# Fewer recurrence tiles beside the cached pages, and a short first group of dense tokens

## The chip, the cores and the metric

One core of a Trainium2 chip runs the whole kernel. The metric is the device time of one execution, in microseconds. TensorE (PE in the profile) does the matrix products and writes to PSUM; PEld is its loading of weights. VectorE is DVE, ScalarE is ACT, GpSimd is POOL. SyncE (SP) computes nothing: it issues most of the DMAs, one after the other, and waits before each for what it needs.

## The reference, cut to what matters

One layer of a hybrid decoder, run on a prompt of 2048 tokens and on 8 samples of 4 new tokens each, in 32-bit floats:

- `cols = RMSNorm(x) @ w_in`, split among three head groups.
- Gated delta rule (6 heads of 64): a causal convolution, then a recurrence over chunks of 64 tokens that carries a 64x64 state for each head. Called GDN below.
- Differential attention (4 heads): causal on the prompt; for the samples over 64 cached pages of 128 rows each, found through a page table.
- RWKV7 (6 heads of 64): a second recurrence with a 64x64 state for each head.
- `x += concat(three outputs) @ w_out`; then attention to 256 memory tokens; then a gated feed-forward of width 2816 with a causal convolution of width 3 on the gate; then a final RMSNorm. Caches and states are outputs too.

The recurrences are serial over token tiles. All that follows `w_out` is independent from token to token, but for the convolution, which needs the two tokens before.

## The kernel before, in words

The program is written out by hand. Each piece of work is a *lane*: one Python generator for each engine, which issues the instructions of one slot and yields. The functions `weave` (slots spread evenly) and `merge` (slots put at given places) interleave the lanes of several pieces into one fixed order of instructions on each engine. Engines execute in that order, so a slot that waits holds up all that was put behind it on its engine. Semaphores tie the engines together.

The stages, in order of time:

1. Projection and the prompt's attention (0 to about 1254 us).
2. **Cached pages.** `paged_lanes` reads 512 pages of keys and 512 of values, 128 KB each. SP issues three of four key pages and a part of the value pages, ACT and POOL the rest. Beside it, woven in, run the first `LEAD` token tiles (of 128 tokens) of GDN, then the first `LEAD` of RWKV, then the projection of the memory tokens (`in_turn`, lines 4256 to 4270). `paged_lanes` has 162 slots, a GDN tile 24, an RWKV tile 29, the memory projection 15; both sides are spread evenly over the stage.
3. The recurrences of the samples (to about 2095 us).
4. **Dense groups.** `feed_lanes` takes the 2080 tokens in five groups of `GROUPS` columns. Each group passes all weights once: `op` (w_out, 8 units), `wq`, `sc`/`nrm`/`tp`/`pv` (memory attention, in four sub-tiles of `quarter(c)` tokens), `wo`, `fp` (feed-forward up, 11 quads of 7 units), `fo` (down, 24 units), `ft` (final norm and stores, again by sub-tiles). The `fp` units multiply halves of the group (one level of Strassen: 7 products instead of 8), so their matmuls have `GROUPS[c]/2` columns. A unit's weights are one tile of at most 512 KB, in a ring of `W_RING` = 4. Merged in are the remaining token tiles of both recurrences: `spread` (line 4384) gives each group the tiles that the next group will read, evenly over its own places up to unit `fo` 14. Group 4 has none; the samples' memory attention and closing transposes stand there. `tokens_done` makes SP wait for the tiles' stores before a group's input is loaded.

`GROUPS` sets the shape of two kinds of transfer. With q = `quarter(c)`, a group's tokens are cut in four sub-tiles of q rows (the last group adds one of 32, the samples):

```python
quarter = lambda c: (GROUPS[c] - (NS if c == NCH - 1 else 0)) // 4
...
sp.dma_start(xs[0:q, n % 2, 0:4, :],
             pr.i["x_prompt"][0][t0:t0 + q * 4, at].rearrange("(i p) n -> p i n", p=q))
...
dst = pr.y_p[GROUP_AT[c] + at:GROUP_AT[c] + at + n, :] if n > NS else pr.y_s
sp.dma_start(dst, res[0:n, j % 2, :]).then_inc(stored[j % 2], 16)
```

The first (line 3420) loads the residual input, q partitions of four rows of 512 bytes, once for each `op` unit, two buffers. The second (line 3450) stores a finished sub-tile, n rows of 4096 bytes, from two buffers: ACT fills a buffer again only when its store has landed (`act.wait_ge(stored...)` in `ft`). At the end of the last group these stores are the last work of the program.

Of the kernel before, what the change touches and what calls it, by code (L numbers as in the profile page):

```python
# [39 lines left out]
NEG = -1.0e30  # L40


LEAD = 3
GROUPS = (384, 384, 416, 448, 448)
W_RING = 4
GROUP_AT = tuple(sum(GROUPS[:c]) for c in range(len(GROUPS)))
GROUP_P = GROUPS[-1] - NS
B_QKV, B_Z, B_DIFF, B_RWKV, B_BETA = 0, 9, 12, 18, 29
# [3214 lines left out]
def feed_lanes(nc, st, pr, C):  # L3263
    L = Lanes()
    GM, NA, RING = max(GROUPS), 9, W_RING
    Q = 112
    PARTS = (range(0, 8), range(8, 16), range(16, 22))
    quarter = lambda c: (GROUPS[c] - (NS if c == NCH - 1 else 0)) // 4

# [51 lines left out]
    spare = lambda c: xTs[:, (c + 1) % 2, :, :].rearrange("p k n -> p (k n)")  # L3321
    prob_of = lambda c, j: spare(c)[0:Q, 1024 * (j % 2):1024 * (j % 2) + 1024].rearrange("p (h m) -> p h m", m=MEM)

    def pT_of(c, j):
        cells = spare(c)[:, 2048:2048 + 8 * Q] if j % 2 == 0 else flat[:, 4 * GM:4 * GM + 8 * Q]
        return cells.rearrange("p (c h n) -> p c h n", c=2, h=MH)
    res = flat[0:Q, NA * GM - 2048:NA * GM].rearrange("p (u d) -> p u d", u=2)
    rstd = st.sb("f_rstd", [P, GM])
# [18 lines left out]
    def tokens(c):  # L3347
        G, H = GROUPS[c], GROUPS[c] // 2
        sums_of = lambda n: spare(c)[:, n * 2 * GM:(n + 1) * 2 * GM].rearrange("p (k n) -> p k n", k=4)[:, :, 0:H]
        one, two = slice(0, H), slice(H, G)  # L3350
        return dict(a11=h[:, 0:4, one], a12=h[:, 4:8, one], a21=h[:, 0:4, two], a22=h[:, 4:8, two],
                    s1=sums_of(0), s2=sums_of(1), s3=h[:, 0:4, two], s4=sums_of(2))

    def temps(c):
        H = GROUPS[c] // 2
        return [spare(c)[:, (6 + n) * GM:(7 + n) * GM].rearrange("p (a n) -> p a n", a=2)[:, :, 0:H] for n in range(2)]
# [112 lines left out]
    def pe_lane(pe):  # L3469
        def step(c, kind, j):  # L3470
# [48 lines left out]
            if kind == "tp":  # L3519
# [3 lines left out]
                for x in range(2):  # L3523
                    u = (kind, c, 2 * j + x)
                    free(pe, u)
                    for hh in range(MH):
                        mm = pe.transpose(bank(u)[:, hh * Q:hh * Q + n], prob[0:n, hh, x * P:(x + 1) * P], pr.ident[0:n, 0:n])
                    mm.then_inc(E.sem[kind], 1)
            if kind == "pv":
# [4 lines left out]
                for hh in range(MH):  # L3534
                    for x in range(2):
                        mm = pe.matmul(bank(u)[:, hh * Q:hh * Q + n], C.mV[:, x, hh * MHD:(hh + 1) * MHD], pT[:, x, hh, 0:n],  # L3536
                                       start=(x == 0), stop=(x == 1))
# [34 lines left out]
    def act_lane(act):  # L3572
# [14 lines left out]
        def step(c, kind, j):  # L3587
# [26 lines left out]
            if kind == "tp":  # L3614
# [5 lines left out]
                for x in range(2):  # L3620
                    u = (kind, c, 2 * j + x)
                    E.wait(act, "tp", c, 2 * j + x)
                    act.activation(pT[:, x, :, 0:n], bank(u)[:, 0:4 * Q].rearrange("p (h n) -> p h n", n=Q)[:, :, 0:n], ACT.Copy)\
                       .then_inc(E.sem["ptk"], 1)
# [208 lines left out]
def memory_lanes(nc, st, pr, F, banks, recurrences):  # L3833
# [24 lines left out]
    def clear(eng):  # L3858
        for lane in recurrences:
            eng.wait_ge(lane.stored, 16 * (TILES - LEAD))  # L3860

# [106 lines left out]
def closing_lanes(nc, st, pr, C, F, banks, recurrences, jobs, stores, f_rows, f_stores):  # L3968
# [8 lines left out]
    def clear(eng):  # L3977
        for lane in recurrences:
            eng.wait_ge(lane.stored, 16 * (TILES - LEAD))

# [51 lines left out]
def build(nc, ins, outs, upto=99):  # L4032
# [12 lines left out]
    with Stage(nc) as st:  # L4045
# [22 lines left out]
        with Stage(nc) as ds:  # L4068
# [131 lines left out]
            with Stage(nc) as ms:  # L4200
# [51 lines left out]
                with Stage(nc) as ps:  # L4252
                    K_ = paged_lanes(nc, ps, pr, A_)
                    banks = [ps.ps(f"shared{j}", [P, 512]) for j in range(3)]
                    with Shared(ps, banks) as gs:
                        D_ = gdn_lanes(nc, gs, pr, S_g, C, 0, LEAD)
                    with Shared(ps, banks) as rs_:
                        R_ = rwkv_lanes(nc, rs_, pr, S_r, C, 0, LEAD)
                    with Shared(ps, banks) as ms_:
                        W_ = memory_project_lanes(nc, ms_, pr, C, g_kv)  # L4260
                    loads_in, r_in = ps.sem("loads_in"), ps.sem("r_in")
                    done = ((D_.stored, 16 * LEAD), (r_in, 16 * len(r_loads)))
                    n_slots = D_.slots + R_.slots + W_.slots
                    last = ((R_.stored, 16 * LEAD),)
                    turns = lambda eng, one, two, three: (
# [84 lines left out]
                with Stage(nc) as ls:  # L4350
# [6 lines left out]

                    C.tokens_done = tokens_done
                    F_ = feed_lanes(nc, ls, pr, C)
                    banks = [ls.ps(f"bank{j}", [P, 512]) for j in range(6)]  # L4360
                    with Shared(ls, banks) as first:
# [121 lines left out]
```

## Time and profile before

| what | value |
|---|---|
| runs, median of 3 | 5283.54 us (5266.91 to 5286.02) |
| the profiled execution, its own time | 5274.61 us |
| its span, first to last instruction | 5273.0 us |
| PE busy | 4786.2 us, 91% of the span |
| PE weight load busy | 3456.9 us, 66% |
| DVE busy | 2540.1 us, 48% |
| ACT / POOL busy | 1408.7 us, 27% / 837.3 us, 16% |
| TensorE's mean granted clock | 0.943 of full |
| HBM read / written | 541.70 MB / 72.16 MB |

The profile is one execution, and all rows below come from it. A busy share over the whole span mixes stages with different limits, so the rows are taken by stage.

### The profile page before, as it was taken

Reading aid. Unit: us, or ns where it says so; the run is one execution under the profiler, and the core shown is the slowest. Engines: PE = TensorE matmul, PEld = TensorE weight load, DVE = VectorE, ACT = ScalarE, POOL = GpSimd, SP = SyncE. Lnnn points to the kernel's source line nnn. Section 1 sums busy time; section 2 is a strip of 40 time slices with the busy share of each in tenths; the row PEclk is TensorE's granted clock in tenths of the full one; section 3 lists DMA queues with packets and bytes.
Section 4 is the critical chain, followed back from the end, with each engine's and each line's share of the span. In section 5 each row is a group of like instructions: output and inputs, shape, how many; then the busy total and the mean of one; then the engine's idle time right before and its main releaser. Section 6 shows DMA issues by size and latency. Waiting matters only on the chain. (4 is left out here: it accounts for less than half of the span.)

```text
span 5273.0 us, 99191 instructions
## 1 busy us (share of the span) xinstructions
PE 4786.2 (91%) x38490; PEld 3456.9 (66%) x38490; DVE 2540.1 (48%) x5724; ACT 1408.7 (27%) x3230; POOL 837.3 (16%) x1111
## 2 busy tenths in 40 slices
PE   8888999997777878999999999989999899999998
PEld 5544445554545555687776877768776597757885
DVE  1136666663445524466545655446453464412442
ACT  3224544552223312222213222132121321112111
POOL 3422221212232210111011110210101101010000
PEclk9999999998888875999999999989999899997999
DMA  6631111114777733144342433424443243342443
GB/s 214 223 98 34 40 37 37 39 37 124 217 230 234 240 116 68 54 138 130 122 119 63 137 123 120 123 56 143 124 125 102 64 135 105 123 146 72 152 143 96
DMA packets 684224, 620.34 MB, mean 118 GB/s; under 512 B 82759, under 2 KB 637255, under 8 KB 683724
## 3 DMA queue, kind: packets, MB, share of 16 engines
q1 hardware_dynamic: 610990, 517.16, 32.6%
q10 hardware_dynamic: 60480, 63.27, 3.7%
q0 software_dynamic: 12288, 33.57, 2.1%
q8 instruction: 307, 5.03, 0.4%
q14 instruction: 159, 1.30, 0.1%
HBM read 541.70 MB, written 72.16 MB: 116 GB/s over the span
## 5 line engine op out<-in xcount | busy, mean ns | idle before, releaser
L3485 PE MATMUL s_f_b<-s_arena 128*128 128x192 f32 (+2 forms) x3520 | 668.5, 346 | 14.3 <-DVE s_arena L3673 7.7
L3485 PEld LDWEIGHTS s_f_b<-s_arena 128*128 128x128 f32 x3520 | 620.4, 192 | 33.2 <-issue 18.3
L3555 PE MATMUL s_f_b<-s_f_a,s_arena 128*128 128x384 f32 (+2 forms) x1760 | 635.0, 517 | 1.5 <-DVE s_f_a L3721 1.5
L581 PE MATMUL s_p_acc<-s_hT,s_p_W 128*128 128x416 f32 x1600 | 606.5, 526 | 6.5 <-DMA s_p_W<-in_w_in_dram 6.5
L3555 PEld LDWEIGHTS s_f_b<-s_f_a,s_arena 128*128 128x128 f32 x1760 | 330.0, 191 | 264.5 <-issue 173.9
L3485 PE MATMUL s_f_b<-s_f_xT,s_arena 128*128 128x192 f32 (+2 forms) x2640 | 495.7, 342 | 0.1
L3485 PEld LDWEIGHTS s_f_b<-s_f_xT,s_arena 128*128 128x128 f32 x2640 | 460.0, 190 | 8.5 <-issue 1.4
L581 PEld LDWEIGHTS s_p_acc<-s_hT,s_p_W 128*128 128x128 f32 x1600 | 297.9, 195 | 245.6 <-issue 232.0
L3495 PE MATMUL s_f_b<-s_arena 128*128 128x384 f32 (+2 forms) x960 | 355.6, 524 | 12.4 <-PEq L124 9.3
L3769 DVE TENSOR_TENSOR s_f_xT<-s_f_xT,s_f_b 128x384 f32<-128x384 f32 (+2 forms) x160 | 93.9, 587 | 498.7 <-PE s_f_b L3555 423.4
L3817 POOL TENSOR_TENSOR s_f_ex<-s_f_ex,s_f_mix 128x384 f32<-128x384 f32 (+2 forms) x105 | 112.2, 1069 | 1272.5 <-ACT s_f_mix L3585 1272.3
L3495 PEld LDWEIGHTS s_f_b<-s_arena 128*128 128x128 f32 x960 | 180.8, 193 | 156.1 <-issue 108.9
L934 ACT ACTIVATE s_prob<-s_s_ps,s_ntop 128x512 f32<-128x512 f32 (+3 forms) x320 | 196.4, 620 | 303.7 <-DVE s_ntop L989 303.6
L3658 ACT ACTIVATE s_f_ex<-s_f_ex 128x384 f32<-128x384 f32 (+2 forms) x110 | 60.5, 550 | 488.4 <-DVE s_f_ex L3707 488.4
L1224 PE MATMUL s_tp<-s_ident,s_K 128*128 128x128 f32 x1024 | 162.7, 307 | 27.7 <-DMA s_K<-in_cache_diff_k_dram 13.4
L1198 POOL DMA_DIRECT2D s_arena<-in_cache_diff_v_dram x256 | 138.8, 542 | 258.5 <-issue 256.3
L986 DVE TENSOR_REDUCE s_ntop<-s_s_ps 128x2 f32<-128x1024 f32 (+3 forms) x160 | 169.7, 1060 | 20.0 <-PE s_s_ps L878 17.7
L1224 PEld LDWEIGHTS s_tp<-s_ident,s_K 128*128 128x128 f32 x1024 | 128.8, 157 | 48.7 <-issue 17.2
L878 PE MATMUL s_s_ps<-s_kT,s_qT 32*128 32x512 f32 (+3 forms) x640 | 82.9, 588 | 69.9 <-ACT s_prob L934 69.8
L1066 POOL TENSOR_SCALAR s_prob<-s_prob,s_alpha 128x512 f32<-128x512 f32 (+3 forms) x160 | 102.4, 654 | 249.3 <-DVE s_alpha L1016 246.0
L3219 POOL TENSOR_TENSOR s_g_zg<-s_g_zt,s_norm_g 128x384 f32<-128x384 f32 x16 | 17.4, 1087 | 769.5 <-DVE s_g_o L3103 738.0
L1412 DVE COPY s_kT<-s_tp 128x512 f32<-128x512 f32 x128 | 88.1, 688 | 87.1 <-PE s_tp L1224 86.5
(813 smaller groups left out, 8069.4 us busy)
## 6 DMA issues: line engine op xcount, KB each, us to landing
s_arena<-w_sums SPq DMA_DIRECT2D x220, 512.0 KB, 3.3
s_arena<-in_ffn_w_in_dram SPq DMA_DIRECT2D x165, 512.0 KB, 3.6
s_K<-in_cache_diff_k_dram SPq DMA_DIRECT2D x384, 128.0 KB, 3.1
s_arena<-in_ffn_w_out_dram SPq DMA_DIRECT2D x80, 512.0 KB, 4.0
s_arena<-in_cache_diff_v_dram POOLq DMA_DIRECT2D x256, 128.0 KB, 3.8
s_arena<-in_cache_diff_v_dram ACTq DMA_DIRECT2D x192, 128.0 KB, 3.6
s_parts<-in_ffn_w_in_dram SPq DMA_DIRECT2D x88, 256.0 KB, 4.4
w_sums<-s_parts SPq DMA_DIRECT2D x44, 512.0 KB, 2.9
```

Source lines behind the costliest of these rows:

```text
L581: mm = pe.matmul(self.acc[n % 2][:, 0:CH], self.W[:, u, k, :], self.hT[:, k, c * CH:(c + 1) * CH], start=(k == 0), stop=(k == KD - 1))
L934: e = act.activation(prob[:, slot(n, c), r, 0:wd], s_ps[hh][:, m, 0:wd], ACT.Exp, scale=scale, bias=ntop[:, u, c, r:r + 1], accum_out=den[ ...
L986: dve.tensor_reduce(ntop[:, u, c, 2 * hh:2 * hh + 2], s_ps[hh][:, :, 0:wd], AX.X, ALU.max)\
L1066: m = pool.tensor_scalar(prob[:, k, 2 * hh + 1, 0:wd], prob[:, k, 2 * hh + 1, 0:wd], alpha[:, n % 2, c, 2 * hh + 1:2 * hh + 2], 1.0, ALU.m ...
L1198: pool.dma_start(V_[:, g % VG, i, :], vp[page_of(pool, g, i)].rearrange("a p h d -> p (a h d)"))\
L1224: mm = pe.transpose(dst[:, i, :], K[:, g % KG, i, h * P:(h + 1) * P], pr.ident[:, :])
L1412: dve.tensor_copy(kT[:, g % 6, 1, :], src[:, :, :].rearrange("p i n -> p (i n)"))\
L3485: mm = pe.matmul(out[:, x, :], w[:, k, x, :], right[:, k, :], start=(k == 0), stop=(k == 3))
L3495: mm = pe.matmul(bank(u)[:, 0:G], w[:, k, :], h[:, k, 0:G], start=(k == 0), stop=(k == KD - 1 and kind != "op"))
L3555: mm = pe.matmul(bank(u)[:, 0:G], w[:, k, :], a[:, f % NA, 0:G], start=(k == 0), stop=(k == len(part) - 1))
L3769: dve.tensor_tensor(x, x, bank(u)[:, 0:G], ALU.add).then_inc(E.sem[kind + "k"], 1)
L3817: pool.tensor_tensor(acc, acc, sq[:, m % 2, 0:GROUPS[c]], ALU.add).then_inc(E.sem["add"], 1)
```

## The change

The number of token tiles of each recurrence that run beside the cached pages goes from three to two; the third tile of GDN and the third of RWKV run in the dense stage. The groups become one of 256 tokens and four of 456. `Q`, the stride of a head in the banks of the memory attention, follows the largest sub-tile.

```diff
-LEAD = 3
-GROUPS = (384, 384, 416, 448, 448)
+LEAD = 2
+GROUPS = (256, 456, 456, 456, 456)
...
 def feed_lanes(nc, st, pr, C):
     L = Lanes()
     GM, NA, RING = max(GROUPS), 9, W_RING
-    Q = 112
+    Q = 114
```

What follows from it by the code's own arithmetic: the sub-tiles `quarter(c)` go from 96, 96, 104, 112, 104 rows to 64, 114, 114, 114, 106. The token tiles that `spread` puts beside groups 0 to 3 go from 3, 4, 3, 3 to 4, 4, 3, 3. The slots woven against the 162 of the cached pages go from 174 to 121. No function is added.

## Rows read from the trace of the kernel before

**Rows 1.** Windows by stage: length, busy (instructions) of each engine, PE clock, DMA, GB/s.
```profile
1254.00:1917.00 663.00, 486.24 (x6409) 339.95 (x6409) 304.87 (x649) 169.83 (x323) 191.46 (x312) 0.85 0.73 219
1917.00:2095.00 178.00, 142.88 (x943) 107.95 (x943) 63.23 (x160) 26.40 (x74) 6.84 (x11) 0.65 0.35 73
2095.00:5250.00 3155.00, 3031.45 (x26110) 2366.96 (x26110) 1535.53 (x3433) 688.78 (x1494) 328.84 (x325) 0.97 0.37 113
```

**Rows 2.** Waits of SyncE, 1254 to 1770 us: total us, times, longest.
```profile
SPq L1154 <- PE s_tp L1224: 32.9, 17, 7.9
```

**Rows 3.** The same in 1270 to 1470 us.
```profile
SPq L1154 <- PE s_tp L1224: 1.0, 2, 0.8
```

**Rows 4.** SyncE's issues in order of time: six key pages.
```profile
1409.99 5.85 SPq L1161 DMA_DIRECT2D s_K<-in_cache_diff_k_dram  x6
```

**Rows 5.** The recurrences' banks in the stage of the pages, same columns, no POOL.
```profile
1269.00:1900.00 631.00, 160.71 (x3544) 131.62 (x3544) 79.87 (x186) 34.14 (x73) 0.86 0.74 223
```

**Rows 6.** End of the stage in order of time: last RWKV output, memory projection's first matmul.
```profile
1907.72 0.49 ACT L2650 ACTIVATE s_r_oT<-s_shared 128x384 f32<-128x384 f32 x1 [4.42 <-PE s_shared L2639]
1917.57 1.94 PE L1578 MATMUL s_shared<-s_ident,s_w_x 128*128 128x128 f32 x8 [9.89 <-ACT s_w_x L1566]
```

**Rows 7.** The recurrences' banks beside groups 0 to 3, 13 tiles of each.
```profile
2095.00:4666.00 2571.00, 599.05 (x15431) 511.99 (x15431) 343.18 (x806) 152.90 (x325) 0.98 0.37 111
```

**Rows 8.** The dense banks in group 0 (384 tokens) and group 4 (448).
```profile
2095.00:2728.00 633.00, 457.89 (x2036) 340.47 (x2036) 66.68 (x121) 23.77 (x65) 0.98 0.37 113
4666.00:5272.00 606.00, 524.71 (x2102) 390.40 (x2101) 74.31 (x121) 36.76 (x85) 0.93 0.39 120
```

**Rows 9.** Runs of matmuls at full clock with 192, 224 and 128 columns.
```profile
2331.01 5.47 PE L3485 MATMUL s_f_b<-s_arena 128*128 128x192 f32 x32
4931.99 6.22 PE L3485 MATMUL s_f_b<-s_arena 128*128 128x224 f32 x32
1953.57 14.46 PE L1589 MATMUL s_shared<-s_w_W,s_w_mT 128*128 128x128 f32 x128
```

**Rows 10.** Ends of two GDN tiles that follow each other fastest, in group 1.
```profile
2777.28 0.47 ACT L3048 ACTIVATE s_g_oT<-s_bank 128x384 f32<-128x384 f32 x1
2908.26 0.49 ACT L3048 ACTIVATE s_g_oT<-s_bank 128x384 f32<-128x384 f32 x1
```

**Rows 11.** That stretch: all engines.
```profile
2777.00:2908.00 131.00, 117.55 (x1498) 85.13 (x1496) 78.04 (x173) 44.23 (x112) 25.43 (x25) 0.97 0.23 64
```

**Rows 12.** PE's waits there: longest in total, and the largest by a recurrence.
```profile
PE s_f_b L3508 <- POOL s_f_ex L3817: 7.3, 2, 4.8
PE s_bank L2431 <- ACT s_r_rs L2650: 1.0, 1, 1.0
```

**Rows 13.** DMA, 5254 to 5267 us: packets, queue with share of 16 engines, issues.
```profile
DMA packets 516, 1.84 MB, mean 141 GB/s; under 512 B 68, under 2 KB 68, under 8 KB 516
q1 hardware_dynamic: 516, 1.84, 50.7%
out_dram<-s_f_a SPq DMA_DIRECT2D x4, 416.0 KB
out_dram<-s_f_a SPq DMA_DIRECT2D x1, 128.0 KB
```

**Rows 14.** DMA, 1970.5 to 1973.5 us: two stores of 128 partitions alone.
```profile
DMA packets 544, 1.05 MB, mean 350 GB/s; under 512 B 32, under 2 KB 32, under 8 KB 544
q1 hardware_dynamic: 544, 1.05, 93.8%
```

**Rows 15.** DMA, 4666 to 4718 us, the `op` units of group 4, packets of 512 bytes.
```profile
q1 hardware_dynamic: 10142, 5.05, 36.6%
```

**Rows 16.** Two `op` units of group 4, and the last stores, in order of time.
```profile
4665.76 6.28 PE L3495 MATMUL s_f_b<-s_arena 128*128 128x448 f32 x16
4673.18 6.28 PE L3495 MATMUL s_f_b<-s_arena 128*128 128x448 f32 x16
5254.74 9.49 SPq L3450 DMA_DIRECT2D out_dram<-s_f_a  x5
```

## The prediction

> **What bounds the kernel now.** I read the busy table by stage first, then in each stage the waits of the engine that issues or computes last, then the transfers at the end.
>
> In the dense stage PE is busy 3031 of 3155 us [rows 1]: whatever is added to PE there is paid in full. In the stage of the cached pages PE is busy 486 of 663 us, DMA 73% of its time, DVE less than half [rows 1], so none of these fills it. SP does nearly: six key pages take 5.85 us from the first start to the last end [rows 4], 1.1 us a page, so that its 384 key and 64 value pages are 493 us, before the states and tiles that it loads too. What SP waits for PE before it gives out a page is 32.9 us in 516 [rows 2], and 1.0 us in the 200 from 1270 on [rows 3]. The stage is paced by SP's issues most of the time and by PE the rest. After the last page a serial piece stands alone: the last RWKV output at 1907.7 us, its store, and the memory projection's first matmul at 1917.6, 9.9 us idle [rows 6].
>
> **The change part by part.** All against the profiled execution (5274.6 us; the median of the runs is 8.9 us above it).
>
> *One tile of each recurrence leaves the pages.* Three tiles cost PE 160.7 us there at a mean clock of 0.86 [rows 5], one 53.6. What that gives back is bounded by who paces. From below: if SP's issues set all, only the tile's own loads and the overlap at the end, some 15 us. From above: all of PE's 53.6 us, a third of its stalls on recurrence results (20, an estimate: of its 175 idle us in the stage about a third), and the end piece, some 90 us. Between: SP's waits for PE are 33 us, of which I take 25, since one third of the woven work goes but the order keeps the rest; the stretch after the last key page, where the RWKV chain and the last values' products alternate, has a third fewer RWKV slots in it, 8 us; and the last tile now ends before slot 142 of 162, beside the products of the last pages, so that its closing norm and store, ahead of the 9.9 us idle [rows 6], are half hidden, 10 us. I take 43 us less, the ends being 15 and 90.
>
> *The tile arrives in the dense stage.* 599.05 us for 13 tiles [rows 7] are 46.1 us of PE each, on an engine with no room: plus 46 us.
>
> *Closer recurrence slots in group 0.* Dense work on PE is 457.9 us at 384 tokens and 524.7 at 448 [rows 8], 1.04 us a token with little fixed beside 57 us; 256 tokens come to about 325. Up to unit `fo` 14, some 86% of it by the units' count of matmuls, group 0 is then 280 us and four tiles of 46: 464 us, 116 us a tile, where the same sum gives 177 for three tiles before. The fastest tile in the trace took 131 us [rows 10], and there PE was idle 13.4 us [rows 11], of which the largest wait on a recurrence is 1.0 and the largest of all, 7.3, is the group's own sum of squares [rows 12]. DVE was busy 60% there. So the chains can run at that spacing; for 10% closer I add 2 us a tile, 8 us, between 0 and 40 (10 us a tile, what the woven recurrences show in the stage of the pages at 105 us a tile).
>
> *Other matmul widths.* The pitch is 5.47/32 = 171 ns at 192 columns, 194 at 224, 113 at 128 [rows 9]; the loads of weights hide at 128 too. The columns streamed are the same in sum (1040 halves), and 113 + 4 x 197 is 901 against 171 + 171 + 182 + 194 + 194 = 912, times 1232 matmuls: 13 us less at best, nothing if the pitch at 228 is 200. I take 0. A weight tile of 512 KB then lasts 16 x 113 ns = 1.8 us on PE in group 0, but with the recurrence slots between some 3 us, and with three loads ahead that is hidden; uncovered it would be up to 2 us a tile of the 77.
>
> *Rows that don't divide.* Here stands the one cost outside PE's sum. In the last 13 us the only transfers are four stores of 104 rows and one of 32, and beside 448 packets of 4096 bytes (4 x 104 + 32) there are 68 small ones [rows 13]. With one closing packet for each DMA engine used, two stores of 128 partitions have 32, 16 each [rows 14]; 68 is 4 x 13 + 16. So 104 rows went over 13 engines, 8 rows each, and 32 over 16: the number is one that divides the rows, the largest up to 16. For 114 rows it is 6, for 106 it is 2. The Trainium skill, "DMA: Bandwidth & Descriptors", section "Why a DMA increments its semaphore by 16 and not by 1", says just this: the largest k up to 16 that divides the slowest dimension of both sides. By that rule the sum is the one below; the trace agrees (68 small packets).
>
> - The last four stores: 50.7% of 16 engines over 13 us is 105 us for 516 packets, 204 ns each [rows 13]; two stores alone ran at 45 us for 544 packets of 2048 bytes, 83 ns, or 165 for 4096 [rows 14]. Four stores of 53 packets on each of two engines are 212 x 165 to 204 ns = 35 to 43 us, and ACT's next sub-tile waits for them, two buffers behind. The first is issued at 5254.7 us [rows 16], and all five are over before 5267 [rows 13], 9 to 10 us of flow for what will take 35 to 43: plus 26 to 34 us, I take 30. Nothing is left beside it to hide it.
> - The residual loads of group 4: packets of 512 bytes take 0.366 x 16 x 52 / 10142 = 30 ns [rows 15]. 106 rows are 212 packets on each of two engines, 6.4 us, and these also carry 64 of each weight tile, 1.9: 8.3 us for an `op` unit that lasts 7.4 [rows 16] and will last 7.55. Eight units: 6 us, less what the two buffers absorb; I take 3, between 0 and 20.
> - With 114 rows a store is 19 packets on an engine, 4 us, and a load 76 x 30 ns = 2.3 us; both are hidden in groups 1 to 3, where the sub-tiles are spread between other units.
>
> **Sum:** -43 + 46 + 8 + 0 + 30 + 3 = +44 us, 5319 us for the profiled execution; halfway to the runs' median, 5323 us.
>
> **The rivals.**
>
> A. *The thin stores don't come.* 106 rows go over many engines by some other split. For it: only 104, 128 and 32 were seen. Against: 8 rows on each of 13 engines instead of 7 on 15 is a split that nobody would choose but by divisors. Sum +11, 5290 us.
>
> B. *Group 0 is bound by its chains.* Up to `fo` 14, 40% of PE's time there would be recurrence against 26% before; DVE does the two convolutions of a quad in one go, and a recurrence result queued behind them comes too late for PE's next slot. If each of the four tiles loses 14 us more, the sum is +100, 5379 us. For it: a tile every 105 us is all that the stage of the pages reaches, with one recurrence at a time. Against: PE's waits in the fastest tile [rows 11, 12].
>
> C. *The pages were paced by PE.* The stage gives back 90 us or more, with the clock (0.85 there) recovering. Against 46 for the tile and 26 for the stores it turns the sign from 72 us on; at 100 us, no stalls in group 0 and 26 for the stores the sum is -25, 5254 us, faster. Against: SP hardly waits for PE in the first 200 us of pages [rows 3].
>
> **How the numbers follow.** The forecast 0.66, its own range 5290 to 5350; A 0.13; B 0.13; C 0.08. What the measurement can tell from no change is 0.5%, 26 us: 5257 to 5310. Of the forecast 0.54 lies above, of B all, of A a little: slower 0.69. Same 0.25 (the rest of the forecast and most of A), faster 0.06. The range 5280 to 5370 leaves out C, the top of B and a little of the rest.
>
> **What would show it.** The stage of the pages ends 30 to 55 us earlier; if under 20, SP alone paced it, if over 75, C. From the first `op` copy of group 0 to the next group's about 560 us (was 633), with PE idle under 40; over 70 is B. PE busy in the banks of the recurrences over groups 0 to 3 is 645 us. In the last 60 us: four stores of 424 KB with few small packets (4 x 2 + 16 = 24), DMA at 2/16 of its engines, ACT waiting for the stores about 10 us each, and from the first of them to the end some 48 us (was 18). If the small packets are 76 or more, the split is another and A holds.

## The result, and the profile after

The changed kernel takes 5369.9 us (median; 5354.8 to 5378.5) against 5284.8 us of the kernel before in the same comparison: 1.0164 times as long, 95% interval 1.0139 to 1.0189. The profiled execution has a span of 5376.9 us, 103.9 us more than before's 5273.0. The forecast was 5323 us: slower, as measured, but by 38 us, less than half of the measured 85.

Where the span grew, by windows of the profile after (length, busy time and instructions of PE, PEld, DVE, ACT and POOL, granted clock, DMA share, GB/s). The first line is cached pages with the samples' recurrences, then groups 0 to 4, each from its first `op` copy on ACT:

```profile
1248.30:2047.20 798.90, 577.79 (x6175) 401.78 (x6175) 320.56 (x699) 177.06 (x352) 181.37 (x306) 0.80 0.67 196
2047.20:2674.20 627.00, 554.29 (x7743) 485.47 (x7741) 365.64 (x904) 160.71 (x378) 97.66 (x105) 0.92 0.39 118
2674.20:3391.60 717.40, 689.89 (x6582) 522.74 (x6583) 381.70 (x817) 168.24 (x353) 92.26 (x89) 0.98 0.34 103
3391.60:4074.80 683.20, 659.26 (x5636) 496.74 (x5639) 334.89 (x710) 148.80 (x308) 73.99 (x72) 0.98 0.35 106
4074.80:4729.00 654.20, 631.71 (x4909) 475.96 (x4909) 304.60 (x640) 132.04 (x271) 57.03 (x55) 0.97 0.34 106
4729.00:5376.90 647.90, 582.81 (x2472) 445.79 (x2471) 204.82 (x489) 108.51 (x241) 24.08 (x21) 0.91 0.36 112
```

The same six windows of the kernel before:

```profile
1241.40:2095.00 853.60, 629.15 (x7353) 447.90 (x7352) 370.72 (x822) 197.26 (x399) 198.30 (x323) 0.80 0.64 187
2095.00:2728.00 633.00, 610.27 (x6563) 485.61 (x6564) 347.71 (x781) 151.20 (x331) 87.48 (x88) 0.98 0.37 113
2728.00:3379.50 651.50, 619.46 (x6586) 493.27 (x6590) 362.54 (x817) 160.59 (x354) 88.94 (x89) 0.98 0.37 113
3379.50:4021.20 641.70, 615.59 (x5637) 477.89 (x5638) 323.65 (x710) 144.45 (x309) 72.10 (x72) 0.98 0.37 112
4021.20:4665.90 644.70, 622.64 (x4909) 474.53 (x4910) 301.83 (x640) 131.12 (x272) 56.66 (x55) 0.98 0.35 107
4665.90:5273.00 607.10, 572.03 (x2471) 441.52 (x2471) 202.66 (x489) 107.05 (x241) 23.66 (x21) 0.93 0.39 120
```

Read length minus PE busy as PE's idle time. The pages are 54.7 us shorter. Group 0 has two thirds of the tokens and is only 6 us shorter: its idle time went from 22.7 to 72.7 us and its clock from 0.98 to 0.92. Groups 1 to 3 carry more tokens, with as little idle time as before (73.9 us against 80.2). Group 4 has 65.1 us idle against 35.1. What stands before the pages ended 6.9 us later, with the same instructions; in all eighteen profiles of this document it ends between 1237.3 and 1251.5 us, so this is scatter.

What PE waited for in group 0 (line, releaser, total us, times, longest), the six largest:

```profile
PE s_bank L2639 <- DVE s_r_o L2720: 13.8, 4, 3.8
PE s_f_b L3485 <- DVE s_f_val L3796: 13.6, 3, 6.3
PE s_bank L2584 <- DVE s_r_APk L2792: 8.6, 2, 4.7
PE s_f_b L3527 <- DVE s_f_a L3759: 5.5, 1, 5.5
PE s_bank L2969 <- DVE s_g_kq L3103: 4.6, 3, 3.1
PE s_bank L3037 <- DVE s_g_o L3103: 4.0, 3, 2.7
```

All six end on DVE, though DVE is busy only 58% of the group: 50.1 us, five of them on recurrence work or on a bank whose release stands behind it. In group 0 of before the first of these was 3.9 us and the second was not in the list.

By banks, the recurrences in group 0 and in groups 1 to 3 (answering [rows 7]), then the dense banks in groups 0 and 4 (answering [rows 8]):

```profile
2047.00:2674.00 627.00, 224.02 (x5710) 190.12 (x5706) 124.75 (x292) 57.59 (x121) 0.92 0.39 118
2674.00:4729.00 2055.00, 428.09 (x10905) 367.12 (x10905) 245.14 (x576) 107.77 (x229) 0.98 0.34 105
2047.00:2674.00 627.00, 347.11 (x2036) 296.26 (x2036) 51.54 (x121) 20.45 (x65) 0.92 0.39 118
4729.00:5376.00 647.00, 531.04 (x2103) 390.45 (x2102) 75.25 (x121) 37.18 (x85) 0.91 0.36 112
```

The fourteenth tile brought 53.1 us (652.1 against 599.05).

The last stores, DMA from 5330 us to the end (packets, queue share of 16 engines, issues), and what ACT's copies into the two row buffers waited for:

```profile
DMA packets 481, 1.88 MB, mean 40 GB/s; under 512 B 24, under 2 KB 24, under 8 KB 480
q1 hardware_dynamic: 480, 1.87, 10.6%
out_dram<-s_f_a SPq DMA_DIRECT2D x4, 424.0 KB
out_dram<-s_f_a SPq DMA_DIRECT2D x1, 128.0 KB
```

```profile
5344.71 1.09 ACT L3653 ACTIVATE s_f_a<-s_f_b 106x512 f32<-106x512 f32 x2 [8.99 <-DMA out_dram<-s_f_a]
5352.96 1.08 ACT L3653 ACTIVATE s_f_a<-s_f_b 106x512 f32<-106x512 f32 x2 [7.16 <-DMA out_dram<-s_f_a]
5361.19 1.07 ACT L3653 ACTIVATE s_f_a<-s_f_b 32x512 f32<-32x512 f32 x2 [7.15 <-DMA out_dram<-s_f_a]
```

24 small packets are 4 x 2 + 16, where [rows 13] had 68: two DMA engines for a store of 106 rows, sixteen for 32. The copies come 8.2 us apart, 155 ns for each of 53 packets. From the first of the last stores to the end it is 42.9 us, against 18.2.

### The profile page after: what moved, and what is told of

The parts are those of the page before. It is cut to its first block and busy times, and to the rows that moved or that the text cites. A ratio compares the mean times of both kernels' runs of the same rounds, so it can differ in the third digit from the quotient of the medians.

```text
span 5376.9 us, 99189 instructions
## 1 busy us (share of the span) xinstructions
PE 4821.9 (90%) x38490; PEld 3469.3 (65%) x38490; DVE 2543.3 (47%) x5724; ACT 1412.8 (26%) x3230; POOL 836.9 (16%) x1111
## 5 line engine op out<-in xcount | busy, mean ns | idle before, releaser
L3485 PE MATMUL s_f_b<-s_arena 128*128 128x228 f32 (+1 forms) x3520 | 676.1, 349 | 27.0 <-DVE s_f_val L3796 15.8
L3555 PE MATMUL s_f_b<-s_f_a,s_arena 128*128 128x456 f32 (+1 forms) x1760 | 635.9, 517 | 1.4 <-DVE s_f_a L3721 1.4
L3485 PE MATMUL s_f_b<-s_f_xT,s_arena 128*128 128x228 f32 (+1 forms) x2640 | 499.8, 344 | 0.8 <-ACT s_f_xT L3633 0.8
L3495 PE MATMUL s_f_b<-s_arena 128*128 128x456 f32 (+1 forms) x960 | 360.2, 530 | 14.6 <-PEq L124 9.3
L3769 DVE TENSOR_TENSOR s_f_xT<-s_f_xT,s_f_b 128x456 f32<-128x456 f32 (+1 forms) x160 | 94.0, 588 | 532.1 <-PE s_f_b L3555 443.1
L3817 POOL TENSOR_TENSOR s_f_ex<-s_f_ex,s_f_mix 128x456 f32<-128x456 f32 (+1 forms) x105 | 111.9, 1066 | 1232.5 <-ACT s_f_mix L3585 1232.5
L3658 ACT ACTIVATE s_f_ex<-s_f_ex 128x456 f32<-128x456 f32 (+1 forms) x110 | 60.4, 549 | 487.8 <-DVE s_f_ex L3707 487.8
L3219 POOL TENSOR_TENSOR s_g_zg<-s_g_zt,s_norm_g 128x384 f32<-128x384 f32 x16 | 17.4, 1088 | 817.4 <-DVE s_g_o L3103 786.1
L1285 PE MATMUL s_o_ps<-s_arena,s_PT 128*32 128x256 f32 x1024 | 82.2, 475 | 61.2 <-DMA s_arena<-in_cache_diff_v_dram 60.5
```

Source lines behind the costliest of these rows:

```text
L3485: mm = pe.matmul(out[:, x, :], w[:, k, x, :], right[:, k, :], start=(k == 0), stop=(k == 3))
L3495: mm = pe.matmul(bank(u)[:, 0:G], w[:, k, :], h[:, k, 0:G], start=(k == 0), stop=(k == KD - 1 and kind != "op"))
L3555: mm = pe.matmul(bank(u)[:, 0:G], w[:, k, :], a[:, f % NA, 0:G], start=(k == 0), stop=(k == len(part) - 1))
L3769: dve.tensor_tensor(x, x, bank(u)[:, 0:G], ALU.add).then_inc(E.sem[kind + "k"], 1)
L3817: pool.tensor_tensor(acc, acc, sq[:, m % 2, 0:GROUPS[c]], ALU.add).then_inc(E.sem["add"], 1)
```

## Experiments

All against the kernel before on the same chip; "own" is the median. The kernel before had a median of 5275.0 to 5284.8 us in these comparisons, so a difference of two "own" times carries up to 10 us of that; the ratios don't. Group 0's length and PE idle time are from each kernel's profile.

| run | own us | ratio, 95% interval | group 0 us | idle us |
|---|---|---|---|---|
| the change | 5369.9 | 1.0164 (1.0139 to 1.0189) | 627.0 | 72.7 |
| e1 split stores | 5340.8 | 1.0111 (1.0088 to 1.0135) | 626.6 | 67.2 |
| e2 and split loads | 5349.3 | 1.0130 (1.0107 to 1.0153) | 625.4 | 70.9 |
| e3 narrow taps | 5359.2 | 1.0147 (1.0123 to 1.0170) | 617.1 | 64.0 |
| e4 LEAD 3, new groups | 5333.7 | 1.0099 (1.0074 to 1.0124) | 527.4 | 32.0 |
| e5 before, LEAD 4 | 5328.0 | 1.0086 (1.0069 to 1.0103) | 575.9 | 17.9 |
| e7 before, 106-row tail | 5313.9 | 1.0070 (1.0053 to 1.0086) | 632.8 | 22.7 |
| e9 before, slots squeezed | 5317.2 | 1.0075 (1.0058 to 1.0092) | 664.0 | 46.0 |
| e10 no convolution | 5357.7 | 1.0153 (1.0136 to 1.0170) | 613.8 | 63.0 |
| e11 = e1, convolutions apart | 5339.2 | 1.0094 (1.0071 to 1.0118) | 628.9 | 62.7 |
| e12 = e1, slots spread | 5341.0 | 1.0112 (1.0091 to 1.0134) | 584.9 | 54.2 |
| e13 = e4, split stores | 5310.8 | 1.0053 (1.0036 to 1.0071) | 527.4 | 30.3 |
| e14 = e13, LEAD 4 | 5354.0 | 1.0140 (1.0118 to 1.0162) | 466.6 | 23.1 |
| e15 = e1, half a slot apart | 5366.9 | 1.0156 (1.0134 to 1.0178) | 630.7 | 71.2 |
| e16 before, half a slot apart | 5317.0 | 1.0067 (1.0049 to 1.0084) | 649.2 | 30.5 |
| e17 = e1, more dense work | 5367.7 | 1.0175 (1.0144 to 1.0207) | 655.2 | 40.7 |
| e18 before, more dense work | 5378.4 | 1.0185 (1.0164 to 1.0205) | 731.1 | 19.8 |

### The thin transfers: e1, e2, e7

```diff
-                sp.dma_start(dst, res[0:n, j % 2, :]).then_inc(stored[j % 2], 16)
+                cuts = [0, 96, n] if c == NCH - 1 and n > 96 else [0, n]
+                for lo, hi in zip(cuts, cuts[1:]):
+                    sp.dma_start(dst[lo:hi, :], res[lo:hi, j % 2, :]).then_inc(stored[j % 2], 16)
```

(the waits on `stored` count two for one in the last group; e2 cuts the loads of line 3420 in the same way; e7 is the kernel before with `GROUPS = (384, 384, 416, 440, 456)`.)

> The kernel after, with each 106-row store of the last group given out as two, of 96 and of 10 rows. Theory 1 (a store of 106 rows is served by 2 DMA engines, and the last sub-tiles wait for it): the stretch from the first of the last stores to the end falls from 43 us to 15 to 20 us, ACT's 23 us of waits for a free row buffer go, and the time is 24 to 30 us less than that of the kernel after, about 5343 us. Rival (the tail is long for another reason, as the lower clock there): less than 8 us, 5362 us or more. Nothing before the last sub-tiles changes.

> As the run with split stores, and the eight 106-row loads of residual x of the last group also in two parts, 96 and 10 rows. If those loads held PE up (my term was 3 us, 0 to 20), it is 3 to 9 us faster than with the stores split alone; if they are hidden, the same within 2 us, or a little slower for eight more issues on SP.

> The kernel before with the last two groups 440 and 456 tokens instead of 448 and 448, so that the last group's sub-tiles have 106 rows (and group 3's 110), nothing else. Theory (2 DMA engines for 106 rows): the stretch from the first of the last stores to the end grows from 18 to 43 us, the time by 24 to 30 us, 5299 to 5305 us. Rival (the tail costs so only together with the other group sizes or the moved tile): within 8 us of the kernel before.

Theory 1 held in e1: 29.1 us faster than the change, and from the first of the last stores to the end 17.7 us. DMA of e1's last 20 us:

```profile
DMA packets 577, 1.88 MB, mean 94 GB/s; under 512 B 120, under 2 KB 120, under 8 KB 576
q1 hardware_dynamic: 576, 1.87, 32.6%
```

The same bytes, and 120 small packets: 4 x 16 for 96 rows, 4 x 10 for 10, 16 for 32. In e7 the tail alone was put on the kernel before: 42.9 us from the first of the last stores, the same 23.3 us of ACT's waits as after the change, and the time is 34 us up, 4 to 10 more than I expected. The residual loads (the 106-row loads of line 3420) were hidden: with them split too, group 4's idle time is 40.4 us against 41.6. The time is no better; it is 8.5 us up, more than the 2 us I had allowed, but the two intervals overlap, and in the profiles PE's busy time in group 4 makes up the difference (591.6 against 581.0 us, at a clock of 0.91 against 0.93).

### The number of tiles beside group 0: e4, e13, e14, e5

One line each: `LEAD = 3` (e4, e13) or `LEAD = 4` (e14) in the changed kernel, `LEAD = 4` in the kernel before (e5). e13 and e14 have the split stores, so they compare with e1.

> Three tiles of each recurrence beside the pages as in the kernel before, with the groups of the kernel after (256, 456 x4): 3 tiles instead of 4 in the 256 tokens of group 0, and the thin transfers of the last group stay. Theory (density in group 0 costs the excess): PE idle in group 0 falls from 73 to about 40 us, mean clock there to 0.95 or more, banks of s_f_b in group 0 from 347 to about 335 us; against the kernel before +30 for the stores, +3 for the loads, about +15 for group 0: 5325 to 5335 us. Rival (a group of 256 tokens is costly by itself, whatever stands beside it): idle in group 0 stays above 60 us and s_f_b there at 345, 5355 us or more.

> The groups 256 and four of 456 with three tiles beside the pages and split stores: both named costs gone, the moved tile and the thin stores. If these two (29 us for the stores, 36 for the moved tile) add up, 5333.7 - 29 = 5305 us; what is left against the kernel before, 20 to 30 us, would be the group sizes themselves and what the rows of the runs show of the clock there. If they overlap, above 5315 us.

> Groups of 256 and four of 456, split stores, four tiles of each recurrence beside the pages: 2 tiles beside group 0, where 3 took 527.4 us and 4 took 626.6 us for the group, PE idle 30.3 and 67.2 us. Theory D (the price climbs as the slots close up): the step from 2 to 3 tiles is 50 to 60 us, against 99 from 3 to 4, so group 0 takes 467 to 477 us with 18 to 26 us idle. Rival (each tile costs the same 99 us in a group this narrow): 430 to 440 us. The stage of the pages grows by about 100 us as in the other run with four tiles there; total 5340 to 5360 us.

> The kernel before with four tiles of each recurrence beside the pages instead of three, groups unchanged: group 0 has 2 tiles beside it. From the two LEAD values measured so far with equal groups (a tile in the pages 55 to 66 us, in a crowded group 0 about 100, in an uncrowded one about 46 plus its stalls): if a tile's price in the dense stage is what its neighbours leave it, here where group 0 is roomy a tile moved out gives back only 46 to 55 us and costs 55 to 66 in the pages, 5275 to 5295 us. If the pages still had room for it (my term of 43 us for a tile) it would be even or faster, 5262 to 5275 us.

Group 0 of 256 tokens with two, three and four tiles beside it (e14, e13, e1), all engines; then for each the recurrences' banks and the dense ones:

```profile
2209.00:2675.60 466.60, 443.48 (x5376) 390.82 (x5375) 263.84 (x665) 121.06 (x290) 65.97 (x72) 0.97 0.50 150
2209.00:2675.60 466.60, 128.18 (x3339) 108.12 (x3339) 72.26 (x168) 33.92 (x71) 0.97 0.50 150
2209.00:2675.60 466.60, 329.33 (x2037) 283.91 (x2036) 51.42 (x121) 20.20 (x65) 0.97 0.50 150
```

```profile
2097.50:2624.90 527.40, 497.13 (x6552) 436.68 (x6552) 313.45 (x781) 138.67 (x331) 81.65 (x88) 0.95 0.45 136
2097.50:2624.90 527.40, 175.40 (x4516) 148.88 (x4516) 98.18 (x230) 45.42 (x96) 0.95 0.45 136
2097.50:2624.90 527.40, 339.04 (x2036) 288.55 (x2036) 51.39 (x121) 20.24 (x65) 0.95 0.45 136
```

```profile
2042.00:2668.60 626.60, 559.45 (x7742) 489.79 (x7738) 365.47 (x904) 160.23 (x378) 97.74 (x105) 0.92 0.39 118
2042.00:2668.60 626.60, 228.45 (x5706) 193.24 (x5702) 124.70 (x292) 57.36 (x121) 0.92 0.39 118
2042.00:2668.60 626.60, 347.73 (x2036) 297.30 (x2036) 51.48 (x121) 20.51 (x65) 0.92 0.39 118
```

The third tile costs 60.8 us (53.7 of PE's busy time, 7.1 idle), the fourth 99.2 (62.3 busy, 36.9 idle). The third lines hold one and the same dense work, and it takes 329.3, 339.0 and 347.7 us as the clock falls from 0.97 to 0.92: the stalls also make the work behind them slower, as the longest one below shows in single rows. This is the price of the step that failed. It is not the price of a narrow group, as e4's rival had it. Taking the stores as known, e1 against e13 is the move of the tile alone: 30 us slower (36 from e4 to the change), 99.2 us more in group 0 against 64 less in the stage of the pages. e13's 5310.8 us lie between my two conditions (5305 if the costs add up, above 5315 if they overlap); split stores are worth 23 us there.

The pages' side climbs too. From the end of the projection to the first `op` copy, the nine profiles with two tiles there give 790 to 803 us, the seven with three 854 to 865, the two with four 962 and 964 (e5 and e14). So the third tile cost 63 us in the mean, 54.7 in the pair first compared, and the fourth 103. e5 gained 57.1 us in its group 0 and lost those 100: 45 us slower, beyond what I expected of it.

### What makes the stalls: e9, e17, e18

e9, the kernel before with the slots of group 0's three tiles squeezed:

```diff
-                            places += [start + (end - start) * (k + 0.5) / n for k in range(n)]
+                            stop = F_.place(c, "fp", 42) if c == 0 else end
+                            places += [start + (stop - start) * (k + 0.5) / n for k in range(n)]
```

e17 (the change with split stores) and e18 (the kernel before), more dense work on PE in group 0:

```diff
-                for x in range(2):
+                for x in ((0, 0, 1) if c == 0 else (0, 1)):
                     for k in range(4):
```

> The kernel before with its group 0 of 384 tokens and 3 tiles, but the slots of these tiles spread up to the first product of quad 6 (57% of the group's plan) instead of output block 14 (73%): a tile then about every 135 to 145 us instead of 180, near the 131 to 138 of the kernel after; the rest of the group has no recurrence beside it. Theory D (the spacing of the slots makes the stalls, whatever the group's width): PE idle in group 0 rises from 23 to 45 to 60 us, time at half clock from 24 to 60 to 90 us, the kernel is 30 to 50 us slower. Rival W (units of 128 columns on PE, short against DVE's fixed costs, make them): idle stays under 32 us and the time within 10 us.

> The kernel after with split stores (5340.8 us; group 0 626.6 us, PE idle 67 us, 102 us at half clock), where in group 0 each unit of the first feed-forward product does its first four matmuls twice (the result is the same): 308 more matmuls of 128 columns at 113 ns, 34.8 us more work on PE, nothing more on another engine. Theory D (PE runs out of dense work between slots while DVE and ACT are still at the chains): the extra work fills idle time and the clock falls less often: group 0 grows by 5 us less to 15 us more, PE idle falls to 35 to 50 us. Rival (the stalls come at fixed places, whatever PE has to do in between): idle stays above 60 us and group 0 grows by 28 to 38 us.

> The same doubling in group 0 of the kernel before (633.0 us, 22.7 us idle, 24 us at half clock): 308 matmuls of 192 columns at 171 ns, 52.7 us. By both theories there is little idle time to fill: group 0 grows by 42 to 55 us. If it grew by less than 30 us, PE would not be what bounds that group and the reading of the kernel before would be wrong.

Group 0 of e9, e17 and e18:

```profile
2110.70:2774.70 664.00, 618.04 (x6563) 496.18 (x6560) 346.87 (x781) 150.92 (x331) 87.15 (x88) 0.95 0.36 108
```

```profile
2031.40:2686.60 655.20, 614.52 (x8360) 547.55 (x8357) 365.30 (x904) 160.38 (x379) 98.14 (x105) 0.95 0.37 113
```

```profile
2108.20:2839.30 731.10, 711.34 (x7180) 586.02 (x7178) 348.36 (x781) 152.62 (x332) 87.12 (x88) 0.98 0.32 98
```

e9 shows the placing of the slots alone at work: same groups, same instructions, and group 0 of the kernel before grows by 31.0 us, its idle time doubles, its clock falls from 0.98 to 0.95. Theory D held. But the GDN tiles end 157 and 168 us apart (182 and 180 before), not the 135 to 145 that I expected, and those two intervals hold 18.1 and 15.9 us idle, as much as the 131 to 138 us intervals of the change do (17.4, 19.5, 17.2), while e13's of 148 and 144 us hold 9.7 and 4.8. Closer slots make more idle time in one and the same group; the microseconds between two tiles don't by themselves say how much.

In e17 and e18 I had counted the added work too low by half: each matmul of the program stands as two in the trace, so it is 618 more in e17 (8360 against 7742), 70 us at 113 ns, and 617 in e18, 105 us at 171 ns. Of the 70 us, 28.6 show in group 0's length, and idle time falls from 67.2 to 40.7 us with the clock back at 0.95: 41 us of extra work cost nothing (26.5 us of it is idle time filled, the rest the faster clock). (The 28.6 lie in the rival's window, but that window was set for 34.8 us of work; the idle time tells the two apart, and it is D's.) Of the 105 us in the kernel before, 98.1 show: there PE bounds the group. So in group 0 after the change PE runs out of dense work between the slots.

### What does not make them: e3, e10, e11, e12, e15, e16

e3 and e10 shorten DVE's convolution in group 0; e11 moves the second convolution of a quad behind the bank's release (`if i == 6 and not c: conv(c, 2 * q + 1)`); e12 spreads the slots (`end` at `fo` 18, `inputs` at `fo` 20, group 0 only); e15 and e16 put RWKV's slots half a slot later (`(k + 1.0) / n` for it).

> The kernel after, where the second and third tap of the dense convolution work on 2 columns instead of 256 in group 0 alone (those parts of the computation are left out): 44 DVE instructions go from about 0.48 us, some of them 1.1 us, to about 0.15 us, 15 to 25 us of DVE work in group 0, nothing on PE. Theory Q (in group 0 recurrence results stand in DVE's in-order queue behind the dense convolutions): PE idle in group 0 falls from 73 us to 45 to 55, the clock there rises from 0.92, and the time is 20 to 45 us less. Theory L (the recurrence's own chain of steps is too long for four tiles in 520 us, whoever runs it): PE idle stays above 65 us and the time within 8 us of the kernel after.

> The kernel after, where in group 0 all three taps of the dense convolution and its clamp work on 2 columns (those parts of the computation are left out): 176 DVE instructions in group 0 become short, about 35 us of DVE work less; narrowing two of the taps took 11.8 us of it away and gave 9.9 us of group 0. Theory Q (PE's stalls in group 0 are mostly a queue on DVE): PE idle in group 0 falls from 73 to 35 to 50 us and group 0 from 627 to 590 to 600 us. Theory L (the recurrences' own chain of steps sets the rest): idle stays at 58 us or more, group 0 at 608 us or more.

> The kernel after with split stores (5340.8 us) and, in group 0, the second dense convolution of a quad moved from its unit 5 to its unit 6, behind the release of the PE bank: DVE's two convolutions no longer stand in one piece ahead of recurrence results. Theory Q (one piece of 5 us in DVE's queue makes the stalls, as rival B of the prediction put it): PE idle in group 0 falls from 67 to below 50 us, 15 us or more faster, below 5326 us. Theory L (taking 17 us of this work away gave only 13 us of 627, so the pieces are not the main cause; the chains PE, ACT, DVE that stand ahead of a bank's release are): within 8 us, 5333 to 5349 us, and idle above 60 us.

> The kernel after with split stores (5340.8 us) and, in group 0, the four tiles' slots spread up to output block 18 instead of 14 (about 79% of the group's plan instead of 73), with the next group's loads given out at block 20 instead of 16. Theory D (spacing of the slots makes the stalls): a tile every 140 to 145 us instead of 137, PE idle in group 0 before the last block falls by 6 to 12 us and the time at half clock by 10 to 25 us, 8 to 18 us faster; against it the next group's loads (1.9 MB) may now be late by 0 to 8 us at its first product. Net -12, 5329 us. If stalls do not depend on the spacing, nothing falls, and the loads make it 0 to 8 us slower.

> The kernel after with split stores (5340.8 us), and in all groups the RWKV slots half a slot later in the plan than the GDN slots, instead of at the same places. Theory P (the two chains come due in pairs, and DVE and ACT do both while PE has only one or two dense units in between): the waits for s_r_o at the tiles' ends (13 us in group 0) and those behind s_f_val (14 us) shrink, PE idle in group 0 falls from 67 to 35 to 50 us, groups 1 to 3 lose 3 to 8 us each, 20 to 40 us faster in all. Theory L (each chain alone is longer than the dense work between two of its own slots): PE idle in group 0 stays within 8 us and the time within 10 us.

> The same half-slot offset in the kernel before. Theory P: its stalls on recurrences are a third of those in group 0 of the kernel after, so 5 to 15 us faster, 5265 to 5275 us. Theory L: within 5 us.

e3 and e10 took 11.8 and 17.1 us of DVE's work out of group 0 (the short instructions keep a fixed part, so less than I reckoned) and gave 9.9 and 13.2 us. Most of what DVE does not have to do comes back, but 63 of 72.7 us of idle time stay without the convolution: between Q and L, nearer to L. e11 bore out L: idle 62.7 against 67.2 us, the same time. In e12 (its group 0 can't be set beside the others of the table, as fewer slots of the next tiles fall before group 1) the spreading did what theory D says in group 0 and gave nothing in all: the three intervals between the ends of the first four GDN tiles hold 37.8 us idle against 51.2 in e1, but group 1, which has to fit its tiles in a shorter stretch, has 41.7 us idle against 27.5, and groups 0 and 1 together take 1347.4 us against 1343.5. The 8 to 18 us that I expected did not come. e15 and e16 refuted my theory P: the two chains half a slot apart are no better beside group 0. They are also 26 and 34 us worse in all, where theory L allowed 10 and 5: in e16 group 0 is 16.2 us longer and groups 1 to 3 together 17.3. Why slots half a place later cost that much stays open. That the chains come due in pairs is not the trouble.

One stall read closely, DVE's rows in order of time (start, duration), and PE's row that waits:

```profile
2337.43 1.33 DVE L2720 TENSOR_TENSOR s_r_Dx<-s_eye,s_r_G 128x384 f32<-128x384 f32 x1 [0.62 <-POOL s_r_G L2418]
2338.68 0.41 DVE L3789 TENSOR_TENSOR s_f_raw<-s_f_xT,s_f_b 128x256 f32<-128x256 f32 x1
2339.97 0.97 DVE L3690 TENSOR_SCALAR s_f_mix<-s_f_raw,s_f_taps,s_f_bias 128x256 f32<-128x256 f32 x1
2340.98 1.10 DVE L3694 SCALAR_TENSOR_TENSOR s_f_mix<-s_f_raw,s_f_taps,s_f_mix 128x256 f32<-128x256 f32 x1
2342.11 0.48 DVE L3698 SCALAR_TENSOR_TENSOR s_f_mix<-s_f_raw,s_f_taps,s_f_mix 128x256 f32<-128x256 f32 x1
...
2343.77 0.41 DVE L3690 TENSOR_SCALAR s_f_mix<-s_f_raw,s_f_taps,s_f_bias 128x256 f32<-128x256 f32 x1
2344.22 0.48 DVE L3694 SCALAR_TENSOR_TENSOR s_f_mix<-s_f_raw,s_f_taps,s_f_mix 128x256 f32<-128x256 f32 x1
...
2345.48 0.58 DVE L2792 COPY_PREDICATED s_r_APk<-s_mask,s_bank 128x384 f32<-128x384 int32 x1
```

```profile
2346.12 1.12 PE L2584 MATMUL s_bank<-s_r_v,s_r_APk 64*64 64x64 f32 x16 [4.71 <-DVE s_r_APk L2792]
```

Two convolutions stand ahead of the result that PE waits for: rival B as I had put it. The largest wait, 6.31 us at 2318.6, is of the other sort:

```profile
2310.91 0.29 DVE L3707 TENSOR_SCALAR s_f_ex<-s_f_mix 128x256 f32<-128x256 f32 x1
2314.82 0.17 DVE L3131 COPY s_g_gs<-s_bank 128x12 f32<-128x12 f32 x1 [3.61 <-ACT s_g_v L3048]
2315.68 1.06 DVE L2755 TENSOR_TENSOR_SCAN s_r_G<-s_scan,s_r_sig 128x128 f32<-128x128 f32 x3
2318.05 0.41 DVE L3796 TENSOR_TENSOR s_f_val<-s_f_xT,s_f_b 128x256 f32<-128x256 f32 x1
```

PE before and after this stall:

```profile
2310.34 1.95 PE L3485 MATMUL s_f_b<-s_arena 128*128 128x128 f32 x16
2318.61 3.42 PE L3485 MATMUL s_f_b<-s_arena 128*128 128x128 f32 x16 [6.31 <-DVE s_f_val L3796]
```

DVE itself sat idle 3.61 us for a recurrence copy of ACT, did some 3 us of recurrence work, and only then came to the addition that frees the dense bank (L3796). In this place a chain over ACT and DVE is longer than the dense units that PE has in the meantime, 1.95 us each at 128 columns. And behind the stall the same sixteen matmuls take 3.42 us instead of 1.95: the granted clock is 0.5 of full from 2314.7 to 2321.5 us.

## Why the prediction was wrong, step by step

| step | forecast | measured |
|---|---|---|
| pages to dense stage | -43 (15 to 90) | -54.7; -63 in the mean of the profiles |
| what stands before the pages | 0 | +6.9, same instructions |
| the tile on PE | +46 | +53.1 |
| closer slots, idle in group 0 | +8 (0 to 40) | +50.0 |
| dense banks (widths) | 0 | +19.4 |
| idle in groups 1 to 3 | 0 | -6.3 |
| last stores and loads, idle in group 4 | +33 | +30.0 |
| memory banks in group 4, rest | 0 | +5.5 |
| sum | +44 | +103.9 |

**The step that failed is "Closer recurrence slots in group 0".** It was priced at 8 us, at most 40, and cost about 75: 50.0 us idle, 7 us more on the tile, and nearly all of the 19.4 us on dense banks, which is not a matter of widths but of the clock there. Groups 1 to 4 spend 534, 534, 530 and 531 us on 456 tokens; the kernel before has 521.5 and 524.7 on 448, 1.0 us a token more as [rows 8] give. What is left, some 20 us, is group 0: 347 us, where the line through [rows 8] gives 325 and e14, with fewer stalls, has 329.3. So "widths 0" was right. Of the forecast's signs, group 0's 627 us (I said 560) and its 72.7 us idle (over 70 "is B") both spoke for rival B. B's total, +100 us on the profiled execution, is near the measured +103.9, but partly by luck: it held 43 us given back by the pages (54.7 came), nothing for the scatter before them (6.9), 64 us idle in group 0 (50.0) and nothing for the clock (some 26).

Part of the evidence was in my own rows. The fastest tile before took 131 us with 13.4 us idle [rows 10, 11], and the GDN tiles of group 0 after end 131 to 138 us apart. Four times 13.4 is 54 us, or 24 without the 7.3 us of the group's own wait [rows 12], where the three tiles of the kernel before had 18.8 us idle up to 2605 us: 5 to 35 us more. 63.9 came, 45.1 more. So the rows would have made the term larger than 8 us, not large enough. I waved it off because no single wait on a recurrence was over 1.0 us [rows 12]; the idle time was the better measure than the name that the longest wait carried. And I priced idle time alone, not the half-speed clock that follows it, which made up about a third of the cost.

B's mechanism was half right. I had blamed the two convolutions in DVE's queue; without them 63 us of idle time stay. That dense work between the slots is too short for the chains is shown (e9, e14, e17); which of a chain's steps is the longest, and how much of it is the other recurrence's work ahead in DVE's queue, was not tried.

**The pages** gave back more than forecast, in both parts. Up to the issue of the last key page the stage is 32.7 us shorter (590.8 to 558.1 us; 38 in the means of the profiles), where I had 25. Here SP's pace holds as the mechanism. Its waits for PE's release of a key buffer, before and after, in that part:

```profile
SPq L1154 <- PE s_tp L1224: 33.7, 19, 7.9
SPq L1154 <- PE s_tp L1224: 17.5, 14, 4.4
```

That is 16.2 us; its other waits fell by about 8 (for PE's `s_o_ps` 2.1, for the tiles' outputs 3.8, for the page table 2.0) and its own instructions by 7 (416 to 409 us). After the last key page the stage is 21.9 us shorter (262.8 to 240.9), where I had 8 + 10: the last RWKV output comes 51.2 us after that issue instead of 75.5, it is now ahead of the last values' product, and PE's idle time before the memory projection's first matmul is 1.8 us instead of 9.9.

With 63 us given back and about 99 spent in group 0, the move of the tile costs 30 to 36 us; with the 29 us of the stores that is 59 to 65 of the 85 us between the medians. The group sizes as such hold the rest, 19 to 37 us by e13's interval; its profile shows 19.4 us more than before's in the dense stage: 8 idle in group 0, 6 idle in group 4, 8 on dense banks. The 6 us are waits for DMA at the start of group 4: 4.0 to 4.2 us for the first weights of `wq` and 2.3 to 2.5 for the memory's keys in the profiles after, e1, e2 and e13, against 0.7 and none before. As e2 has them too, they are not the thin loads; what makes them was not tried.

**The last stores** were right in mechanism, in count (24 small packets) and in size (+24.7 us in the tail, 30 forecast; 29.1 by e1). By the Trainium skill, "DMA: Bandwidth & Descriptors", section "Why a DMA increments its semaphore by 16 and not by 1", the number of engines is the largest up to 16 that divides the slowest dimension of both sides, here the rows. The traces agree: 96, 10, 32 and 106 rows went over 16, 10, 16 and 2, by the count of small packets. **The residual loads** cost nothing (3 forecast), and neither did the 114-row transfers of groups 1 to 3, as claimed. **Rivals A and C** are out: the stores did come, and the sign did not turn.

No variant beats the kernel before. The nearest, e13, is 0.5% slower.

## What to carry to other kernels

When work is moved beside other work, price the idle time that the trace shows where such work stands closest, over the whole stretch, and not only the waits that bear the moved work's name; add what the clock loses behind the stalls, and expect more at a closer spacing than a looser one shows (here the rows gave 5 to 35 us of idle time, and 50 came). The price of one more piece woven in climbs (61, then 99 us on one side; 63, then 103 on the other), so it must be read at the margin, not as a mean. And when a tile's row count changes, count the DMA engines that it leaves for the transfers that nothing hides, and cut such a transfer in two where the count divides badly.

## What the runs showed of the hardware

- A store of 106 rows of 4096 bytes took 8.2 us on two DMA engines; cut in 96 and 10 rows, the same four stores held ACT up for 3.6 us in all, against 23.3.
- DVE beside GpSimd: in the stall above, three DVE instructions took 1.33, 0.97 and 1.10 us, while the like of them took 0.56, 0.41 and 0.48 us moments later. Five GpSimd instructions of 1.0 us (L2418) ran in that stretch (2336.4 to 2341.8 us), with one gap of 0.5 us. The whole profile after says the same: L3690 on 128x256 took 0.97 to 1.11 us in the four cases that ran mostly beside such an instruction and 0.41 to 0.42 in the other 18, and `s_r_Dx<-s_eye,s_r_G`, always partly beside one, took 1.33 to 1.34 us in all 16. L3789, which reads PSUM, took the same time beside one as without (0.63 us on 128x456, three cases beside). No run took GpSimd's work away, so that GpSimd is the cause is not shown by experiment.
- The same instructions of the pages' stage, with three tiles, took 854 to 865 us in seven profiles. Between the shortest (before) and the longest (e4) PE's busy time differs by 10.0 us with the same matmuls, at a granted clock of 0.80 and 0.79. Terms of under some 10 us there can't be told from one pair of profiles.
